# A transformer layer in split fp32: seven block products for eight also in the input projections of the two feed-forward blocks

## The chip, the cores and the metric

The kernel runs on 1 core of one Trainium2 chip. The number that counts is the device time of one execution in microseconds, the median over runs.

The layer works on 256 tokens of width 2048. Nearly all of its work is matrix products on TensorE (PE in the rows). VectorE (DVE), ScalarE (ACT), GpSimd (POOL) and SyncE (SP), which only issues DMAs here, feed it and carry its results away.

## The reference

The whole is `h + 1/2 post1(SwiGLU_1(pre1(h)))`, then a mixer with two attentions, then a second half-step feed-forward block. The change is in the first product of each SwiGLU:

```python
def swiglu_ffn(x, w_in, w_out):          # x: 256 x 2048 after RMS norm, w_in: 2048 x 11264, w_out: 5632 x 2048
    g, u = jnp.split(x @ w_in, 2, axis=-1)
    return (jax.nn.silu(g) * u) @ w_out

h = h + MACARON_W * rms_norm(swiglu_ffn(rms_norm(h, ffn1_pre_g[l]), ffn1_w_in[l], ffn1_w_out[l]), ffn1_post_g[l])
mix = hybrid_mixer(rms_norm(h, mix_pre_g[l]), w_in[l], b_gate[l], sink_a[l], rpb_b[l], w_up_a[l], w_up_b[l], w_out[l])
h = h + rms_norm(mix, mix_post_g[l])
h = h + MACARON_W * rms_norm(swiglu_ffn(rms_norm(h, ffn2_pre_g[l]), ffn2_w_in[l], ffn2_w_out[l]), ffn2_post_g[l])
```

All inputs and outputs are float32.

## The kernel before, in words

**Split products.** Each operand is split into a rounded part (fp32r, "hi") and the rest ("lo"). A product is then three matmuls: hi by hi, hi by the weights' lo, lo by the weights' hi. The weights stand as the moving operand, 512 columns wide, and 128 tokens of the activations as the stationary one. The results gather in PSUM: `acc` holds four banks of 512 columns (two column blocks, each with two token tiles), `tp` four more.

**Chunks.** A "chunk" is 128 rows of the weights by 512 columns. It costs TensorE six matmuls, three for each of the two token tiles (`half`, L1432 to L1434, called by `chunk`). A column block of the input projection takes 16 chunks. `w_in` of a feed-forward block has 22 column blocks: 11 of the gate and 11 of the up half. The kernel goes through them as 11 pairs: gate block, up block, gate block, and so on, and most pairs run inside a loop (`Fori`) on every engine.

**How a chunk gets to TensorE.** SyncE loads two chunks at a time, a "piece" of 512 KB, into one of four places of `raw`. Its wait is for VectorE to be done with the piece that lay there before. ScalarE rounds a chunk from `raw` to `WH` (`split_hi`, L650), VectorE writes `raw - WH` to `WL` (`split_lo`, L945). `WH` and `WL` have eight places each. So ScalarE can round chunk c once TensorE has finished chunk c - 8 (semaphore `chunk_done`). TensorE waits for `lo_ready` at each chunk. Every engine works its own list in order.

**Between the chunks.** ScalarE applies SiLU to the gate block (L755) and VectorE multiplies by the up block (L1099), then turns the result (L1108) into `Z`. SyncE stores `Z` to memory and fetches it back transposed as `Y`; ScalarE and VectorE split `Y` into `MH`, `ML` (L762, L1115), the operands of the output projection.

**Seven products for eight, so far.** In the output projection (`out_pair`, `superblock`) a block of 256 tokens by 256 rows by two column blocks is computed by the Strassen-Winograd scheme: seven products of a quarter block (three matmuls each, L1465 to L1467) for eight. Sums of the activations are formed by `form_sums`, sums of the weights in `T32`, and after all of them the shared products are added up on VectorE (`fold_products`, L1015, L1022).

What sets the order is written out by hand: a table for the output projection (`out_order`), plain loops for the rest.

Of the kernel before, what the change touches and what calls it, by code (L numbers as in the profile page):

```python
# [34 lines left out]
P = 128  # L35
# [72 lines left out]
C_F2OUT = C_F2IN + FFN_IN_BLOCKS * DC  # L108
# [40 lines left out]
def chunks_through(b):  # L149

    if b == B_QKV:
        return C_QKV + DC + SKEW
    if b in (B_WOUT, B_WOUT + 1):
        return C_WOUT + len(CROSSED) - 4 * (B_WOUT + 1 - b)
    for first_b, c_out in ((B_F2OUT, C_F2OUT), (B_F1OUT, C_F1OUT)):
        if first_b <= b < first_b + OUT_BLOCKS:
            return c_out + OUT_DONE[b - first_b]
    for first_b, first_c, chunks in ((B_F2IN, C_F2IN, DC), (B_WOUT, C_WOUT, DC), (B_UP, C_UP, 8),
                                     (B_QKV, C_QKV, DC), (B_F1IN, C_F1IN, DC)):
        if b >= first_b:  # L160
            return first_c + (b - first_b + 1) * chunks


def piece_of(c):

    return c // 2 if c < C_QKV else (c - EXTRA) // 2


def ops_through(piece):

    for c_out, first in ((C_F1OUT, C_F1OUT // 2), (C_F2OUT, piece_of(C_F2OUT))):
        if first <= piece < first + 2 * PAIR_PIECES:
            pair, p = divmod(piece - first, PAIR_PIECES)
            side, k, o, at = [x for x in OUT_PLACES[pair] if x[3] <= p][-1]
            return c_out + pair * PAIR_OPS + o + (4 if side == 2 else 2)
    return 2 * piece + 2 + (EXTRA if piece >= piece_of(C_QKV) else 0)


def supers_through(piece):

    count = 0
    for first in (C_F1OUT // 2, piece_of(C_F2OUT)):
        for pair in range(2):
            count += sum(side == 2 and first + pair * PAIR_PIECES + p <= piece for side, k, o, p in OUT_PLACES[pair])
    return count

# [23 lines left out]
def layer_kernel(nc, x, ffn1_pre_g, ffn1_w_in, ffn1_w_out, ffn1_post_g, mix_pre_g, w_in, b_gate,  # L210
# [4 lines left out]
    with ctx:  # L215
# [53 lines left out]
        prob = [place("prob_b", [P, TT, SEQ], F32)[0],  # L269
                place("prob_a", [P, TT, SEQ], F32, o_mask)[0]]  # L270
# [4 lines left out]
        rpad, _ = place("rpad", [B_H * RPB_USED, PADW], F32, o_yl + 8192)  # L275
# [6 lines left out]
        S32, _ = place("S32", [P, 2, 4, P], F32, o_yl + 12288)  # L282
        T32, _ = place("T32", [P, 4, NB], F32, o_xh + DC // 2 * SEQ * 4)
# [40 lines left out]

        fold = fg[:, :, :].rearrange("p t (j s) -> p (t j) s", s=NB)
# [24 lines left out]
        t_ready = sem("t_ready")  # L350

# [31 lines left out]
        def _(sp):  # L383
# [257 lines left out]
        def _(act):  # L641
# [173 lines left out]
            def ffn(c_in, c_out, b_in, b_out, z0, norm, n):  # L815
# [12 lines left out]
                else:  # L828
                    silu_gate(b_in, norm, more=SKEW)
                for c in range(DC):  # L830
                    split_hi(c_in + 2 * DC + c)
                last = DFF // NB - 1
                with act.Fori(1, last) as i:
                    for c in range(DC):
                        split_hi(c_in + DC + c, i * (2 * DC))
                        if c == 5:
                            fetched_hi(Y, z0 - 1, MH, i * 4 - 4, i)
                        if c == 8:
                            silu_gate(b_in, norm, z0, i)
# [879 lines left out]
```

## Time and profile before

| | |
|---|---|
| median of 3 runs | 2018.22 us (2017.36 to 2019.72) |
| the profiled execution | 2017.83 us, its span 2016.0 us |
| TensorE matmuls | 8866, busy 99% of the span |
| VectorE busy | 65% |
| ScalarE busy | 53% |
| mean DMA rate | 222 GB/s |
| granted TensorE clock, mean | 0.999 |

Matmuls overlap: the row of one lasts longer than the distance to the next. So TensorE's pace is read from starts, or from its weight loads (PEld) with the idle time before them, not from the busy time of the matmuls. The first feed-forward input projection runs until about 484 us.

### The profile page before, as it was taken

How to read it: one execution, taken by the hardware profiler on the slowest of the kernel's cores; microseconds unless marked ns; L12 is line 12 of the kernel's file. 1: busy time of each engine (PE TensorE's matmuls, PEld its weight loads, DVE VectorE, ACT ScalarE, POOL GpSimd, SP SyncE). 2: the span in 40 equal slices, each digit the busy share in tenths (PEclk: the TensorE clock that was granted, in tenths of full speed). 3: DMA queues.
4: the chain of work that ended last, by engine and by line, in shares of the span. 5: the costliest groups of instructions: out<-in, count | busy, mean ns of one | idle time of the engine just before them, and what ended most of it. 6: DMA issues, size and time to landing. Idle time of an engine off the chain costs nothing.

```text
span 2016.0 us, 26937 instructions
## 1 busy us (share of the span) xinstructions
PE 2005.9 (99%) x8866; PEld 1661.1 (82%) x8866; DVE 1319.4 (65%) x2059; ACT 1068.3 (53%) x1885; POOL 50.0 (2%) x86
## 2 busy tenths in 40 slices
PE   9999999999999999999999999999999999999998
PEld 7888888888888888888888888888888888888886
DVE  6655555667767776667777676765556655687685
ACT  7545555555555564445444564665555555555553
POOL 1000000000000011110000000000000000000000
PEclk9999999999999999999999999999999999999999
DMA  8787777777665678987878787586766777666564
GB/s 307 225 231 228 216 220 214 225 224 239 199 209 188 220 219 247 283 244 216 230 228 230 218 246 236 177 263 210 217 213 213 222 226 215 211 221 219 182 213 147
DMA packets 262224, 448.08 MB, mean 222 GB/s; under 512 B 17656, under 2 KB 59896, under 8 KB 261760
## 3 DMA queue, kind: packets, MB, share of 16 engines
q1 hardware_dynamic: 257520, 435.09, 70.2%
q0 software_dynamic: 4336, 11.82, 2.9%
q8 instruction: 44, 0.72, 0.1%
q14 instruction: 36, 0.29, 0.1%
q10 hardware_dynamic: 288, 0.16, 0.0%
HBM read 419.47 MB, written 27.51 MB: 222 GB/s over the span
## 4 chain that ended last, share of the span: by engine, by line
PE 98%; DMA 1%; DVE 0%; ACT 0%; SPq 0%; issue 0%; DVEq 0%; ACTq 0%
PE acc L1432 31%; PE acc L1434 31%; PE acc L1433 31%; PE tp L1466 1%; PE tp L1467 1%; PE tp L1465 1%; PE tp L1612 1%; PE tp L1625 1%; PE acc L1466 1%; PE acc L1467 1%; PE acc L1465 1%; DMA turned_blocks<-Zmix 0%; DMA raw<-in_w_out 0%; DMA raw<-in_ffn_w_in 0%; PE tp L1534 0%; DVE h L1152 0%
## 5 line engine op out<-in xcount | busy, mean ns | idle before, releaser
L945 DVE TENSOR_TENSOR WL<-raw,WH 128x512 fp32r<-128x512 f32 x1080 | 730.3, 690 | 537.5 <-ACT WH L650 536.0
L650 ACT ACTIVATE WH<-raw 128x512 fp32r<-128x512 f32 x1080 | 671.0, 630 | 691.6 <-PE acc L1434 591.0
L1432 PE MATMUL acc<-WH,XH 128*128 128x512 f32 x2030 | 794.3, 391 | 0.4 <-DVE WL L945 0.3
L1434 PE MATMUL acc<-WH,XL 128*128 128x512 f32 x2030 | 790.1, 389 | 0.0
L1433 PE MATMUL acc<-WL,XH 128*128 128x512 f32 x2030 | 790.1, 389 | 0.0
L1432 PEld LDWEIGHTS acc<-WH,XH 128*128 128x128 f32 x2030 | 381.1, 188 | 80.0 <-issue 1.1
L1434 PEld LDWEIGHTS acc<-WH,XL 128*128 128x128 f32 x2030 | 381.1, 188 | 79.3
L1433 PEld LDWEIGHTS acc<-WL,XH 128*128 128x128 f32 x2030 | 381.2, 188 | 78.7
L657 ACT ACTIVATE WH<-raw 128x512 fp32r<-128x512 f32 x312 | 188.9, 629 | 126.9 <-PE acc L1434 103.1
L952 DVE TENSOR_TENSOR WL<-raw,WH 128x512 fp32r<-128x512 f32 x280 | 183.0, 688 | 73.0 <-ACT WH L657 72.9
L1432 PE MATMUL acc<-WH,MH 128*128 128x512 f32 x560 | 217.9, 389 | 0.0
L1434 PE MATMUL acc<-WH,ML 128*128 128x512 f32 x560 | 217.9, 389 | 0.0
L1433 PE MATMUL acc<-WL,MH 128*128 128x512 f32 x560 | 217.9, 389 | 0.0
L1432 PEld LDWEIGHTS acc<-WH,MH 128*128 128x128 f32 x560 | 105.1, 188 | 22.0
L1434 PEld LDWEIGHTS acc<-WH,ML 128*128 128x128 f32 x560 | 105.1, 188 | 21.7
L1433 PEld LDWEIGHTS acc<-WL,MH 128*128 128x128 f32 x560 | 105.1, 188 | 21.8
L669 ACT ACTIVATE WH<-T 128x512 fp32r<-128x512 f32 x64 | 40.5, 632 | 61.4 <-PE acc L1434 56.4
L959 DVE TENSOR_TENSOR WL<-T,WH 128x1024 fp32r<-128x1024 f32 x32 | 39.2, 1225 | 33.7 <-ACT WH L669 33.7
L1432 PE MATMUL acc<-WH,YH 128*128 128x512 f32 x128 | 50.0, 390 | 0.0
L1433 PE MATMUL acc<-WL,YH 128*128 128x512 f32 x128 | 49.8, 389 | 0.0
L1434 PE MATMUL acc<-WH,YL 128*128 128x512 f32 x128 | 49.8, 389 | 0.0
L1108 DVE STREAM_TRANSPOSE Z<-tmp 128x512 f32<-128x512 f32 x58 | 37.9, 691 | 1.0
(158 smaller groups left out, 1072.6 us busy)
## 6 DMA issues: line engine op xcount, KB each, us to landing
raw<-in_ffn_w_in SPq DMA_DIRECT2D x350, 512.0 KB, 3.8
raw<-in_ffn_w_out SPq DMA_DIRECT2D x176, 512.0 KB, 3.9
raw<-in_w_in SPq DMA_DIRECT2D x136, 512.0 KB, 5.3
turned_blocks<-Z SPq DMA_DIRECT2D x33, 512.0 KB, 3.1
Y<-turned_blocks SPq DMA_DIRECT2D x132, 128.0 KB, 4.6
raw<-in_w_out SPq DMA_DIRECT2D x32, 512.0 KB, 4.1
raw<-in_w_up_a SPq DMA_DIRECT2D x16, 512.0 KB, 5.0
raw<-in_w_up_b SPq DMA_DIRECT2D x16, 512.0 KB, 4.6
```

Source lines behind the costliest of these rows:

```text
L650: act.activation(weight_hi(c), raw[:, piece_of(c) % RAW, c % 2, :], ACT.Copy).then_inc(hi_ready, 1)
L657: act.activation(weight_hi(op + i), raw[:, piece % RAW, i, :], ACT.Copy).then_inc(hi_ready, 1)
L669: act.activation(weight_hi(op + 4 + i), T32[:, i, :], ACT.Copy).then_inc(hi_ready, 1)
L945: dve.tensor_tensor(weight_lo(c), raw[:, piece_of(c) % RAW, c % 2, :], weight_hi(c).bitcast(F32), ALU.subtract).then_inc(lo_ready, 1)
L952: dve.tensor_tensor(weight_lo(op + i), raw[:, piece % RAW, i, :], weight_hi(op + i).bitcast(F32), ALU.subtract).then_inc(lo_ready, 1)
L959: dve.tensor_tensor(WL[:, at:at + 2, :], two, WH[:, at:at + 2, :].bitcast(F32), ALU.subtract).then_inc(lo_ready, 2)
L1432: pe.matmul(a, hi[:, tok], weight_hi(c), start=first, stop=False, skip_group_check=again)
L1433: pe.matmul(a, hi[:, tok], weight_lo(c), start=False, stop=False, skip_group_check=again)
L1434: return pe.matmul(a, lo[:, tok], weight_hi(c), start=False, stop=last, skip_group_check=again)
L1465: pe.matmul(out, hi, weight_hi(op), start=first, stop=False)
L1466: pe.matmul(out, hi, weight_lo(op), start=False, stop=False)
L1467: return pe.matmul(out, lo, weight_hi(op), start=False, stop=last)
```

## The change

The two input projections now use the seven-product scheme for 4 of the 16 chunks of each column block. A gate block and the up block of the same pair form the two column blocks, the two token tiles the rows, and chunks 0 to 3 two pairs of row chunks (`IN_S = 2`). Eight of the eleven pairs (numbers 2 to 9) are done so, in both feed-forward blocks; pairs 0, 1 and 10 stay as they were (all counted from 0).

- The products for a pair run while the up block of the pair before is computed (`mixed`, order in `MIXED`; "r" is a piece of the up block, "s" one of seven groups of two products). Then the twelve other chunks of the gate block run, then those of the up block, between which the products for the next pair stand. A round of the loop counts 40 steps of the ring of eight places (`LOOP_OPS`); the last group, T4, counts four steps for its two products.
- The shared products are chained in PSUM and not added up at the end. ScalarE copies a bank to another (`copy_bank`, five times a pair), and TensorE adds the next products onto the copy. VectorE adds once (`seed_right`) to give the up block its start.
- Weights for the products are loaded apart, four transfers of 512 KB a pair, into `SL` and `SR` (`load_sums`). VectorE forms four sums of them (`form_t`, 128x1024 each). ScalarE and VectorE split them 1024 columns at a time.
- Sums of the activations are formed once for each feed-forward block, during the gate block of pair 1.
- Two extra matmuls for each feed-forward block write the banks 1 and 2 of `tp` once.

```diff
+IN_S = 2
+LOOPS = PAIRS - 4
+B11, T2, B21, T3, B22, T1, T4 = range(7)
+MIXED = (("r", 0, 0), ("s", B11, 2), ("r", 1, 4), ("s", T2, 6), ("s", B21, 8), ("r", 2, 10), ("s", T3, 12), ("s", B22, 14),
+         ("r", 3, 16), ("s", T1, 18), ("s", T4, 20), ("r", 4, 24), ("r", 5, 26))
+GATE_OPS = 12
+MIXED_OPS = 28
+LOOP_OPS = GATE_OPS + MIXED_OPS
...
@@ sync
+            def load_sums(c, weights, block, part, di=0):
+                sp.wait_ge(lo_ready, c - 4 + LOOP_OPS * di)
+                half = part % 2 * 2
+                src = weights[bass.ds(block + part // 2 * PAIRS, 1), half:half + 2, :, :].rearrange("b c p n -> p (b c) n")
+                sp.dma_start((SL, SR)[part // 2][:, half:half + 2, :], src).then_inc(sums_landed, 16)
...
-                with sp.Fori(1, last) as i:
-                    load(c_in + DC, wi, 0, DC, i + DFF // NB, i * (2 * DC), z0, i)
-                    load(c_in + 2 * DC, wi, 0, DC, i + 1, i * (2 * DC))
+                with sp.Fori(0, LOOPS) as i:
+                    for j in range(6):
+                        load_part(piece + P_LOOP + j, wi, i + 2, 4 + 2 * j, i)
+                        if j >= 2:
+                            load_sums(c_in + O_LOOP, wi, i + 3, j - 2, i)
+                    load_mixed(piece + P_LOOP + 6, wi, i + 2 + PAIRS, z0 + 2, i)
...
@@ scalar
+            def copy_bank(done_at, out, bank, di):
+                act.wait_ge(chunk_done, done_at + LOOP_OPS * di)
+                act.activation(out, tp[:, bank, :], ACT.Copy).then_inc(copied, 1)
...
+            def mixed_hi(c, piece, d, b, norm, units, first, di=0):
+                for kind, j, o in MIXED:
+                    if o == 6:
+                        silu_gate(b, norm, units, di)
+                    if o == 10:
...
+                        copy_bank(c + 4, tp[:, 1, :], 0, di)
...
+                        copy_bank(c + 4, acc[:, left, :], 0, di)
+                    if o == 14:
+                        copy_bank(c + 8, tp[:, 2, :], 1, di)
+                    if o == 20:
+                        copy_bank(c + 14, acc[:, left + 1, :], 2, di)
+                    if o == 26:
+                        copy_bank(c + 20, TX[:, 0, :], 3, di)
...
+                        act.wait_ge(chunk_done, c + o + 2 - WS + LOOP_OPS * di)
+                        at = (c + o) % WS
+                        act.activation(WH[:, at:at + 2, :], operand(j), ACT.Copy).then_inc(hi_ready, 4 if j == T4 else 2)
...
@@ vector
+            def seed_right(c, b, d, di=0):
+                dve.wait_ge(chunk_done, c + LOOP_OPS * di)
+                dve.wait_ge(copied, 5 * (d + 1) + 5 * di)
+                dve.tensor_tensor(acc[:, 2 * (b % 2):2 * (b % 2) + 2, :], tp[:, 1:3, :],
+                                  TX[:, 0, :].unsqueeze(1).broadcast_to([P, 2, NB]), ALU.add).then_inc(seeded, 1)
...
@@ tensor
+            def products(op, group, d, b, di):
+                left = 2 * (b % 2)
+                out = {B11: tp[:, 0, :], T2: tp[:, 1, :], B21: acc[:, left, :], T3: tp[:, 2, :], B22: tp[:, 1, :], T1: tp[:, 3, :],
+                       T4: acc[:, left + 1, :]}[group]
+                if group in (T2, B21, T3, T4):
+                    pe.wait_ge(copied, 5 * d + {T2: 1, B21: 2, T3: 3, T4: 4}[group] + 5 * di)
+                if group == T1 and d:
+                    pe.wait_ge(seeded, d + di)
...
+                for bank in range(1, 3):
+                    pe.matmul(tp[:, bank, :], XH[:, 0, 0:P], weight_hi(c_in + O_MIXED1 - 4), start=True, stop=True)
...
+                with pe.Fori(0, LOOPS) as i:
+                    for j in range(6):
+                        piece(c_in + O_LOOP + 2 * j, b_in + 4, 4 + 2 * j, False, j == 5, i, True)
+                    mixed(c_in + O_LOOP + GATE_OPS, b_in + 5, first + 1, True, i)
```

On TensorE, at the border from the gate block to the up block of a loop round, first before, then of the change a little further on: the group B11 after the first piece of the up block, and the group T2. `tp<-WH,XH` is a product's matmul, `copied` the semaphore of ScalarE's bank copies.

```order
L1525 ISA
L1438 REGISTER_ALU [waits acc_freed0]
L1432 MATMUL acc<-WH,XH 128x512 [waits lo_ready]
L1433 MATMUL acc<-WL,XH 128x512
L1434 MATMUL acc<-WH,XL 128x512
L1432 MATMUL acc<-WH,XH 128x512
L1433 MATMUL acc<-WL,XH 128x512
```
```order
L1662 REGISTER_ALU
L1663 MATMUL tp<-WH,XH 128x512 [waits lo_ready]
L1664 MATMUL tp<-WL,XH 128x512
L1665 MATMUL tp<-WH,XL 128x512
L1662 REGISTER_ALU
L1663 MATMUL tp<-WH,XH 128x512 [waits lo_ready]
L1664 MATMUL tp<-WL,XH 128x512
L1665 MATMUL tp<-WH,XL 128x512
L1673 ISA
L1662 REGISTER_ALU [waits copied]
L1663 MATMUL tp<-WH,MH 128x512 [waits lo_ready]
L1664 MATMUL tp<-WL,MH 128x512
```

Before, a chunk's six matmuls follow each other and the only other wait is for a free bank. Now there are products with three matmuls and a wait of their own, and T2 also waits for ScalarE.

On ScalarE, in the loop around SiLU, first before, then of the change from T2's weights to T3's. `WH<-TX` and `WH<-SL` are the rounding of two chunks of weights at once, `tp<-tp` and `acc<-tp` the bank copies.

```order
L650 ACTIVATE WH<-raw 128x512 [waits chunk_done]
L753 REGISTER_ALU [waits rstd_ready,chunk_done]
L755 ACTIVATE tmp<-acc,rstd 128x512 [waits blocks_turned]
L755 ACTIVATE tmp<-acc,rstd 128x512
L649 REGISTER_ALU
L650 ACTIVATE WH<-raw 128x512 [waits chunk_done]
L649 REGISTER_ALU [waits raw_landed1]
```
```order
L802 ACTIVATE WH<-TX 128x1024 [waits chunk_done,x_ready]
L800 REGISTER_ALU
L802 ACTIVATE WH<-SL 128x1024 [waits chunk_done]
L783 REGISTER_ALU
L772 REGISTER_ALU [waits seeded]
L773 ACTIVATE tp<-tp 128x512 [waits chunk_done]
L785 REGISTER_ALU
L773 ACTIVATE acc<-tp 128x512 [waits chunk_done,acc_freed0]
L753 REGISTER_ALU
L755 REGISTER_ALU [waits raw_landed0]
L756 ACTIVATE WH<-raw 128x512 [waits chunk_done] x2
```

Before, SiLU stands between single chunks. Now each copy stands in ScalarE's list ahead of the rounding of later weights, and waits for TensorE's products.

On VectorE, in the loop around the gate product, first before, then of the change. `TX<-SR,SL` is `form_t` of T1, `acc<-tp,TX` is `seed_right`.

```order
L945 TENSOR_TENSOR WL<-raw,WH 128x512 [waits hi_ready]
L1096 REGISTER_ALU [waits chunk_done]
L1099 SCALAR_TENSOR_TENSOR tmp<-acc,rstd,tmp 128x512 [waits rstd_ready,acc_freed0]
L1099 SCALAR_TENSOR_TENSOR tmp<-acc,rstd,tmp 128x512
L1108 STREAM_TRANSPOSE Z<-tmp 128x4x4x32 [waits acc_freed1]
L1108 STREAM_TRANSPOSE Z<-tmp 128x4x4x32
L944 REGISTER_ALU
L945 TENSOR_TENSOR WL<-raw,WH 128x512 [waits hi_ready]
```
```order
L1272 SCALAR_TENSOR_TENSOR tmp<-acc,rstd,tmp 128x512 [waits rstd_ready,acc_freed0]
L1272 SCALAR_TENSOR_TENSOR tmp<-acc,rstd,tmp 128x512
L1281 STREAM_TRANSPOSE Z<-tmp 128x4x4x32 [waits acc_freed1]
L1281 STREAM_TRANSPOSE Z<-tmp 128x4x4x32
L1119 ISA [waits chunk_done]
L1120 TENSOR_TENSOR acc<-tp,TX 128x1024 [waits copied]
L1095 TENSOR_TENSOR WL<-raw,WH 128x512 [waits hi_ready]
L1095 TENSOR_TENSOR WL<-raw,WH 128x512 [waits hi_ready]
L1107 ISA
L1109 REGISTER_ALU [waits sums_landed]
L1114 TENSOR_TENSOR TX<-SR,SL 128x1024 [waits seeded]
L1114 TENSOR_TENSOR TX<-SR,TX 128x1024 [waits x_ready]
```

The gate product, which stood in the middle of a gate block, now stands after its eighth chunk, followed by the addition into the up block's banks and by the two sums, of which the first waits for the four transfers (`sums_landed`).

## Rows read from the trace of the kernel before

**Rows 1.** The page, part 1: busy us, share of the span, instructions.
```profile
PE 2005.9 (99%) x8866; PEld 1661.1 (82%) x8866; DVE 1319.4 (65%) x2059; ACT 1068.3 (53%) x1885; POOL 50.0 (2%) x86
```

**Rows 2.** Waits of TensorE, whole span: total us, times, longest us.
```profile
PE tp L1635 <- POOL ident L566: 1.5, 1, 1.5
PE acc L1543 <- ACT WH L650: 0.8, 1, 0.8
PE acc L1432 <- DVE WL L945: 0.3, 1, 0.3
```

**Rows 3.** The page, part 4: the chain that ended last, by engine.
```profile
PE 98%; DMA 1%; DVE 0%; ACT 0%; SPq 0%; issue 0%; DVEq 0%; ACTq 0%
```

**Rows 4.** Groups by form, weight loads: busy us, mean ns, idle before them.
```profile
L1433 PEld LDWEIGHTS acc<-WL,XH 128*128 128x128 f32 x2030 | 381.2, 188 | 78.7
L1432 PEld LDWEIGHTS acc<-WH,XH 128*128 128x128 f32 x2030 | 381.1, 188 | 80.0 <-issue 1.1 <-DVE WL L945 0.7
...
L1465 PEld LDWEIGHTS tp<-WH,XH 128*128 128x128 f32 x48 | 9.0, 188 | 1.9
```

**Rows 5.** Timeline of TensorE where superblocks begin: start us, us, what.
```profile
507.05 0.39 PE L1465 MATMUL tp<-WH,MH 128*128 128x512 f32 x1
...
507.73 0.39 PE L1465 MATMUL acc<-WH,MH 128*128 128x512 f32 x1
```

**Rows 6.** Window 484 to 560 us: busy us and counts, clock, DMA share, GB/s.
```profile
484.00:560.00 76.00, 76.00 (x337) 62.98 (x336) 58.73 (x80) 43.82 (x72) 0.58 (x1) 1.00 0.67 217
```

**Rows 7.** Timeline of VectorE in the first loop: start us, us, what [idle before].
```profile
186.15 1.85 DVE L945 TENSOR_TENSOR WL<-raw,WH 128x512 fp32r<-128x512 f32 x3
...
195.12 0.69 DVE L945 TENSOR_TENSOR WL<-raw,WH 128x512 fp32r<-128x512 f32 x1 [0.67 <-ACT WH L650]
196.48 0.69 DVE L945 TENSOR_TENSOR WL<-raw,WH 128x512 fp32r<-128x512 f32 x1 [0.67 <-ACT WH L650]
```

**Rows 8.** Timeline of ScalarE in the first loop.
```profile
204.51 1.25 ACT L755 ACTIVATE tmp<-acc,rstd 128x512 f32<-128x512 f32 x2
```

**Rows 9.** Groups by form, VectorE and ScalarE.
```profile
L945 DVE TENSOR_TENSOR WL<-raw,WH 128x512 fp32r<-128x512 f32 x1080 | 730.3, 690 | 537.5 <-ACT WH L650 536.0
L650 ACT ACTIVATE WH<-raw 128x512 fp32r<-128x512 f32 x1080 | 671.0, 630 | 691.6 <-PE acc L1434 591.0 <-DMA raw<-in_w_in 49.7 <-DMA raw<-in_ffn_w_in 31.3
...
L1108 DVE STREAM_TRANSPOSE Z<-tmp 128x512 f32<-128x512 f32 x58 | 37.9, 691 | 1.0
L1099 DVE SCALAR_TENSOR_TENSOR tmp<-acc,rstd,tmp 128x512 f32<-128x512 f32 x44 | 30.9, 744 | 0.0
...
L967 DVE TENSOR_TENSOR T<-raw 128x1024 f32<-128x1024 f32 x16 | 19.6, 1223 | 16.8 <-DMA raw<-in_ffn_w_out 16.8
...
L1015 DVE TENSOR_TENSOR acc<-acc,fg 128x1024 f32<-128x1024 f32 x4 | 4.9, 1226 | 0.0
...
L868 ACT ACTIVATE YH<-tp 128x256 fp32r<-128x256 f32 x16 | 5.2, 365 | 0.7 <-PE tp L1625 0.7
...
L674 ACT ACTIVATE XH<-S 128x1024 fp32r<-128x1024 f32 x4 | 4.2, 1046 | 0.0
...
L680 ACT ACTIVATE fg<-tp 128x512 f32<-128x512 f32 x4 | 2.3, 581 | 0.0
```

**Rows 10.** Waits of ScalarE over the whole span.
```profile
ACT WH L650 <- DMA raw<-in_ffn_w_in: 31.3, 23, 3.7
```

**Rows 11.** Waits of SyncE's DMA queue over the whole span.
```profile
SPq L387 <- DVE Z L1108: 99.6, 29, 7.0
```

**Rows 12.** Windows, as rows 6: the start, the first loop, ten busy microseconds.
```profile
14.00:30.00 16.00, 16.00 (x72) 13.24 (x72) 10.93 (x20) 12.51 (x30) 0.00 (x0) 1.00 1.06 388
43.60:479.00 435.40, 435.40 (x1923) 360.68 (x1922) 259.28 (x388) 221.51 (x362) 6.98 (x9) 1.00 0.76 221
190.00:200.00 10.00, 10.00 (x46) 8.29 (x45) 5.22 (x8) 4.53 (x8) 0.79 (x1) 1.00 1.03 287
```

**Rows 13.** The page, part 6: DMA issues, KB each, median us to landing.
```profile
raw<-in_ffn_w_in SPq DMA_DIRECT2D x350, 512.0 KB, 3.8
```

More of the change, by code:

```diff
@@ L185, in supers_through, with j_step @@
     return count
+def j_step(group):
+    return {T1: 1, T2: 2, T3: 3, T4: 4}[group]
 def in_second_ring(c):
@@ L1215, in ffn @@
                     if c == 8:
[L1216 to L1226 removed]
+                        gate_times_up(b_out - 3, norm)
@@ new lines, in products @@
+            def products(op, group, d, b, di):
+                left = 2 * (b % 2)
+                out = {B11: tp[:, 0, :], T2: tp[:, 1, :], B21: acc[:, left, :], T3: tp[:, 2, :], B22: tp[:, 1, :], T1: tp[:, 3, :],
[4 more added lines that the diff above has]
+                    pe.wait_ge(seeded, d + di)
+                fresh = group in (B11, T1)
+                for q in range(IN_S):
+                    first, second = XH[:, 2 * q, :], XH[:, 2 * q + 1, :]
+                    first_lo, second_lo = XL[:, 2 * q, :], XL[:, 2 * q + 1, :]
+                    sh, sl = in_sum(MH, q), in_sum(ML, q)
+                    hi, lo = {B11: (first[:, 0:P], first_lo[:, 0:P]), T2: (sh[:, 1, :], sl[:, 1, :]),
+                              B21: (second[:, 0:P], second_lo[:, 0:P]), T3: (sh[:, 2, :], sl[:, 2, :]),
+                              B22: (sh[:, 3, :], sl[:, 3, :]), T1: (sh[:, 0, :], sl[:, 0, :]),
+                              T4: (second[:, P:2 * P], second_lo[:, P:2 * P])}[group]
+                    last = q == IN_S - 1
+                    product(out, op + q, hi, lo, fresh and q == 0, last, di, not fresh).then_inc(
+                        chunk_done, 3 if group == T4 and last else 1)
@@ new lines, in piece, with mixed @@
+            def piece(c, b, k, first, last, di=0, again=False):
+                for i in range(2):
+                    chunk(c + i, b, XH[:, k + i, :], XL[:, k + i, :], first and i == 0, last and i == 1, LOOP_OPS * di, again)
+            def mixed(c, b, d, again, di=0):
+                for kind, j, o in MIXED:
+                    if kind == "s":
+                        products(c + o, j, d, b - 1, di)
+                    else:
+                        if j == 0 and again:
+                            pe.wait_ge(seeded, d + di)
+                        piece(c + o, b, 4 + 2 * j, False, j == 5, di, again)
@@ new lines, in ffn @@
+                for j in range(12):
+                    if j == 6:
+                        pe.wait_ge(seeded, first + LOOPS + 1)
+                    piece(c_in + O_PAIR9 + 2 * j, b_in + j // 6, 4 + 2 * (j % 6), False, j % 6 == 5, 0, True)
+                for side in range(2):
+                    acc_free(b_out - 2 + side)
+                    for c in range(DC):
+                        chunk(c_in + O_PAIR10 + side * DC + c, b_out - 2 + side, XH[:, c, :], XL[:, c, :], c == 0, c == DC - 1)
```

322 lines of the change are left out of this document (221 added, 101 removed).

## The prediction

> **What bounds the kernel now.** I read the page's totals first: TensorE is busy 99% of the span with 8866 matmuls, VectorE 65%, ScalarE 53% [rows 1]. Busy time of matmuls overlaps, so I looked next at what TensorE waited for: 2.6 us in all, in three waits, all near the start [rows 2]. The chain that ended last is 98% TensorE [rows 3]. So the kernel is one unbroken stream of matmuls, and what counts is their number times their distance. The distance comes from the weight loads: (381.2 + 78.7) us over 2030 loads, 0.2266 us each [rows 4]. VectorE's timeline agrees: it follows TensorE chunk by chunk, and two chunks lie 1.36 us apart, six matmuls of 0.2267 us [rows 7]. The reader is to see that VectorE and ScalarE are idle only because they are ahead: both wait for each other or for TensorE (537.5 and 691.6 us of idle time at the splitting of chunks) [rows 9].
>
> **The change, its saving.** A pair of column blocks cost 32 chunks of 6 matmuls, 192. Now it costs 24 chunks of 6 and 14 products of 3, that is 144 + 42 = 186. Six fewer in 8 pairs of 2 feed-forward blocks are 96; two extra in each block give 4 back. Net 92, which is also the difference of the matmuls in the two programs when loop bodies are counted with their rounds: 8866 against 8774. The saving is 96 x 0.2267 = 21.76 us, less 4 x 0.2267 = 0.91 us: 20.85 us. All of it lies on the path that sets the end, provided that TensorE never has to wait for the new steps.
>
> **Does a product keep the distance of 0.2267 us?** It has a wait, and in the loop a register step, for every three matmuls instead of six. Superblocks in the output projection have the same shape: two products start 0.68 us apart, three times 0.227 [rows 5], and their loads give (9.0 + 1.9) / 48 = 0.227 us [rows 4]. The register step is not in those. Chunks in the loop have one in front of the load at L1432, and these loads idled 80.0 us against 78.7 for L1433 [rows 4]. That is 1.3 us over some 1015 waits, 1.3 ns each. 224 new products at that price are 0.3 us; I take 0 and keep 0.3 as the upper end.
>
> The Trainium skill (TensorE: Matmul & The Clock Gate, "The cost: per-tile semaphore tail") says that semaphore increments by matmuls serialize at about 26 ns each. By that rule the six more increments of a pair would cost, as an estimate, 16 x 6 x 0.026 = 2.5 us. The rows of the superblocks show no such lengthening, though each product there increments once, so the sum goes by the rows.
>
> **Do the new steps stay hidden?** I walk one round of the loop. M 0 is the start of the up block on TensorE, where the products for the next pair are mixed in. TensorE's starts follow from 2.72 us for a piece of two chunks and 1.36 us for a group of two products: B11 at 2.72, T2 at 6.80, B21 at 8.16, T3 at 12.24, B22 at 13.60, T1 at 17.68, T4 at 19.04, the last two pieces at 20.40 and 23.12, the next gate block at 25.84, its end at 42.16. A matmul ends 0.16 us after its slot (row of 0.39 us, distance 0.23 [rows 5]); I take 0.2 us until another engine moves.
>
> ScalarE's steps: a chunk 0.63 us (about 0.57 in a row), SiLU 1.25 us for two tiles [rows 8], two chunks of weights at once 1.05 us, a copy out of PSUM 0.58 us [rows 9]. Its list: SiLU until 1.5, T2's weights until 2.5, B21's until 4.0 (it waits for the ring), then B11 is done at 4.3 and the two copies run until 5.4. T2 needs the first at 6.80: hidden. T3's weights until 8.1, third copy (T2 done at 8.4) until 8.9, needed at 12.24. T1's weights until 13.5, fourth copy until 14.4, needed at 19.04; T4's weights until 15.5. Chunks of piece 4: 16.5 to 17.2 and 17.9 to 18.5. Fifth copy (T1 done at 19.2) until 19.8, then the chunks of the last piece at 20.4 and 21.0.
>
> VectorE's steps: 1.22 us for 1024 columns, 0.69 for 512, 0.58 in a row ((1.85 - 0.69) / 2 [rows 7, 9]). The weights' lo are ready: T2 at 3.7, B21 5.2, T3 9.1, B22 11.0, T1 14.8, T4 16.8, piece 4 at 17.9 and piece 5 at 21.2. TensorE wants them at 6.80, 8.16, 12.24, 13.60, 17.68, 19.04, 20.40 and 23.12. The least lead is 1.9 us, at piece 5, because T4 takes four of the eight places of the ring for two products and the fifth copy waits in front of piece 5.
>
> In the gate block (G 0 = M 25.84) VectorE is done with the eighth chunk at G 1.6, then gate product and turning (2 x 0.744 + 2 x 0.691 less overlap, 2.7 us), `seed_right` 1.23 us (as L1015 [rows 9]), two chunks, T1 at G 6.8 to 8.0, two chunks until 9.3, T2's sum until 10.5. TensorE wants the ninth chunk at G 10.9 and the eleventh at 13.6. So what is added on VectorE, about 33 us busy in a round of 42.2, is covered by the ring's lead of eight chunks, 10.9 us.
>
> A copy from PSUM to PSUM by ScalarE is in no row. Bounds: 0.37 us (256 columns from PSUM) and 1.23 us (VectorE, 1024 columns into PSUM) [rows 9]; I take 0.58, the copy of 512 columns to SBUF. At 1.23 the least lead falls to 1.3 us, still no wait. A gain is excluded, since no step of the kernel before goes away with it. In the gate block of pair 1 VectorE also forms the sums of activations (1.22 + 4 x 0.43 us and waits, about 3.2, then 1.22 for their lo). With the rest that is 19.4 of 21.8 us, with the lead of the ring before it: hidden, and in the worst case 1 or 2 us once for each feed-forward block.
>
> **DMAs.** The bytes are the same. But the four transfers of weights for the products are bunched: SyncE's waits free pieces 2 to 5 of the gate block and the four parts between M 19.5 and 25.2. A transfer of 512 KB takes 1.35 us at the 388 GB/s that the start reached; landing takes 3.8 us from issue [rows 12, 13], so 2.45 us lie around it. Eight in a row from 19.6: two until 22.3, six more until 30.4, landed at 32.9, which is G 7.1. T1's sum wants them at 6.8 and can be late until 11.7 before TensorE waits for the eleventh chunk. In the stretch with the relative-position transfers the rate was 287 GB/s [rows 12]: 1.83 us each, landed at G 10.9, still in time. ScalarE did wait for pieces before, up to 3.7 us [rows 10], and TensorE never noticed. The queue's waits for `Z` (99.6 us in 29 [rows 11]) stay, and now stand where pieces are 10 us ahead.
>
> **The sum.** 2017.83 (the profiled execution, span 2016.0) - 21.76 + 0.91 = 1996.98 us. The median of the runs shown is 0.39 us above the profiled one, so 1997.4 us.
>
> **Rivals.**
> - *Small waits in the rounds.* The leads of 1.9 to 2.9 us are eaten here and there, by 0.5 to 1 us in each of 14 loop rounds: +7 to +14 us, 2004 to 2011 us. For it: the walk has three engines and a queue in step, and five copies that wait for products. Against it: every lead is over 1.2 us at the upper bounds. 9 in 100.
> - *The bunched transfers decide, slower than before.* Place: T1's sum on VectorE. At the loop's mean of 221 GB/s [rows 12] each transfer takes 2.37 us, the last lands at G 15.1, and the eleventh chunk is 3.4 us late: 14 x 3.4 = 48 us, about 2045 us. It turns the gain into a loss from 1.49 us a round (20.85 / 14), when a transfer takes 2.12 us, 247 GB/s. Against it: 221 GB/s was the demand, at 0.76 of the engines' time, and not the limit. 5 in 100.
> - *Products run at a longer distance.* With the register step and wait not hidden, 224 products at 10 to 30 ns: +2 to +7 us, 2000 to 2004 us. Against it: rows 4 and 5. 3 in 100.
> - *The clock falls.* Between groups in changing banks TensorE would pause, and the granted clock drop to 1.2 GHz. If the 114 matmuls of each mixed stretch ran so, 16 x 114 x 0.2267 = 413 us more, 2411 us. Against it: in the stretch with superblocks, which go through seven banks, the clock was 1.00 and TensorE had no gap [rows 6]. 1 in 100. The Trainium skill (TensorE: Matmul & The Clock Gate, "A second HAM failure mode: psum-queue depth-cycling") describes this for a kernel that cycles through banks; by that rule the trace disagrees for this kernel.
> - That fewer matmuls go than stated is excluded by the count.
>
> **How the numbers follow.** The forecast has 82 in 100: 1997.4 us, with 1995.5 to 1999.5 from the spread of runs (2017.36 to 2019.72) and the 0.3 us of register steps. To hold 8 in 10 with the parts of the first and third rival that lie near, I let the range reach to 2005. A change under 0.2%, 4 us, can't be told from none here. Faster: 82, 3 and nearly all of 9, and a little less for what I don't see, 0.93; within 0.2%: 0.02; slower: the second and the fourth, 0.05.
>
> **What would show it.** Right: 8774 matmuls; no wait of TensorE on `copied`, `seeded` or `lo_ready` in the loops beyond a few tenths; rounds of 42.2 us, which VectorE's timeline shows between two gate products; ScalarE's copies near 0.58 us; VectorE busy about 33 us of a round. Wrong: idle time before product matmuls on TensorE released by ScalarE (the copies) or VectorE (T1, T4, piece 5); VectorE idle before T1's sum on a DMA for more than 5 us; a granted clock under 1.00; rounds of 43.5 us or more.

## The result and the profile after

The changed kernel takes 1996.88 us (median of 4 runs, 1996.7 to 1999.51) against 2018.22 us before (4 runs, 2017.36 to 2019.72). The ratio is 0.9897, its 95% interval 0.9879 to 0.9914. Forecast were 1997.4 us and a gain of 20.85 us; the medians differ by 21.3 us, the spans of the profiled executions by 21.1 us (2016.0 to 1994.9).

The totals of the profile after, against [rows 1]:

```profile
PE 1985.8 (100%) x8774; PEld 1645.1 (82%) x8774; DVE 1441.5 (72%) x2135; ACT 1127.6 (57%) x1951; POOL 50.1 (3%) x86
```

There are 92 matmuls fewer (8866 to 8774), as counted ahead. VectorE is 122 us busier and ScalarE 59 us, and neither shows in the time. What TensorE waited for, all of it, against [rows 2]:

```profile
PE tp L1878 <- POOL ident L665: 1.5, 1, 1.5
```

One wait is left, at the very start. The two short ones beside it in [rows 2], 1.1 us together, are not there in this execution; they are too small to explain anything: the gain by spans is only 0.25 us above the forecast one, and two executions differ by more (a second profile of the same kernel has a span of 1995.3 us).

The weight loads, from which the pace is read, against [rows 4]; L1630 and L1631 are the plain chunks, L1663 the products, with busy us, mean ns and idle time before them:

```profile
L1631 PEld LDWEIGHTS acc<-WL,XH 128*128 128x128 f32 x1774 | 333.1, 188 | 68.5
L1630 PEld LDWEIGHTS acc<-WH,XH 128*128 128x128 f32 x1774 | 333.1, 188 | 69.1 <-issue 0.5
...
L1663 PEld LDWEIGHTS tp<-WH,MH 128*128 128x128 f32 x144 | 27.0, 188 | 5.6
```

The chunks: (333.1 + 68.5) / 1774 = 0.2264 us, as before. The products: (27.0 + 5.6) / 144 = 0.226 us. So a product with a wait and a register step for every three matmuls keeps the pace.

The new steps, groups by form of the same profile, against [rows 9]:

```profile
L802 ACT ACTIVATE WH<-SL 128x1024 fp32r<-128x1024 f32 x48 | 50.8, 1059 | 25.5 <-PE acc L1632 25.5
...
L1120 DVE TENSOR_TENSOR acc<-tp,TX 128x1024 f32<-128x1024 f32 x16 | 19.2, 1201 | 0.0
...
L773 ACT ACTIVATE tp<-tp 128x512 f32<-128x512 f32 x32 | 18.6, 582 | 7.6 <-PE tp L1665 7.6
L773 ACT ACTIVATE acc<-tp 128x512 f32<-128x512 f32 x32 | 18.5, 580 | 3.8 <-PE tp L1665 3.8
...
L773 ACT ACTIVATE TX<-tp 128x512 f32<-128x512 f32 x16 | 9.6, 598 | 11.6 <-PE tp L1665 11.6
```

ScalarE's copy from PSUM to PSUM took 0.58 us, the value taken from the copy to SBUF; `seed_right` took 1.20 us for 1.23.

One round of the loop on ScalarE, from its timeline: SiLU of one round, the fifth copy, the chunks of piece 5 and of the next gate block, SiLU of the next round.

```profile
204.56 1.27 ACT L890 ACTIVATE tmp<-acc,rstd 128x512 f32<-128x512 f32 x2 [2.17 <-PE acc L1632]
...
223.52 0.60 ACT L773 ACTIVATE TX<-tp 128x512 f32<-128x512 f32 x1 [0.73 <-PE tp L1665]
224.01 3.22 ACT L756 ACTIVATE WH<-raw 128x512 fp32r<-128x512 f32 x6
...
246.72 1.27 ACT L890 ACTIVATE tmp<-acc,rstd 128x512 f32<-128x512 f32 x2 [2.17 <-PE acc L1632]
```

Two SiLUs lie 246.72 - 204.56 = 42.16 us apart, which is 186 x 0.2267. With SiLU taken as 0.2 us behind the start of the up block, M 0 of the prediction is 204.36 (the block's first matmul stands at 204.28, so places read in this way are good to 0.1 us), and the fifth copy starts at M 19.2, as walked. VectorE in the same round:

```profile
224.67 4.91 DVE L1095 TENSOR_TENSOR WL<-raw,WH 128x512 fp32r<-128x512 f32 x8 [1.15 <-ACT WH L756]
...
232.14 1.40 DVE L1272 SCALAR_TENSOR_TENSOR tmp<-acc,rstd,tmp 128x512 f32<-128x512 f32 x2
...
234.81 1.20 DVE L1120 TENSOR_TENSOR acc<-tp,TX 128x1024 f32<-128x1024 f32 x1
...
237.68 1.22 DVE L1114 TENSOR_TENSOR TX<-SR,SL 128x1024 f32<-128x1024 f32 x1 [0.49 <-DMA SR<-in_ffn_w_in]
238.82 1.29 DVE L1095 TENSOR_TENSOR WL<-raw,WH 128x512 fp32r<-128x512 f32 x2
```

The first of the eight chunks at 224.67 is that of piece 5. Its lo is ready at 225.36, M 21.0; TensorE wants it at M 23.12. The lead is 2.1 us, forecast 1.9. The gate block starts at 204.36 + 25.84 = 230.20, so the gate product stands at G 1.9, T1's sum at G 7.5 after 0.49 us of waiting for the last of the four transfers (forecast: landed at G 7.1), and the eleventh chunk is ready at 239.5, G 9.3, 4.3 us ahead of G 13.6. The burst of transfers is plain in two windows of the same stretch, the DMA share and GB/s last, against [rows 12]:

```profile
208.00:226.00 18.00, 18.00 (x81) 14.93 (x80) 13.70 (x18) 13.49 (x22) 0.79 (x1) 1.00 0.37 80
226.00:242.00 16.00, 16.00 (x72) 13.24 (x72) 14.12 (x21) 7.75 (x14) 0.00 (x0) 1.00 1.03 383
```

### The profile page after: what moved, and what is told of

Same layout as the page of the kernel before. It is cut to its first block, busy times and chain, and to the rows that moved or that the text cites. A ratio compares the mean times of both kernels' runs of the same rounds, so it can differ in the third digit from the quotient of the medians.

```text
span 1994.9 us, 26750 instructions
## 1 busy us (share of the span) xinstructions
PE 1985.8 (100%) x8774; PEld 1645.1 (82%) x8774; DVE 1441.5 (72%) x2135; ACT 1127.6 (57%) x1951; POOL 50.1 (3%) x86
## 4 chain that ended last, share of the span: by engine, by line
PE 100%; DVE 0%; DVEq 0%; ACT 0%; issue 0%; POOL 0%; ACTq 0%; POOLq 0%
PE acc L1630 29%; PE acc L1632 29%; PE acc L1631 29%; PE tp L1665 3%; PE tp L1663 3%; PE tp L1664 3%; PE acc L1665 1%; PE acc L1663 1%; PE acc L1664 1%; PE tp L1868 1%; PE tp L1855 1%; PE tp L1878 0%; PE tp L1769 0%; DVE h L1325 0%; PE acc L1778 0%; PE tp L1828 0%
## 5 line engine op out<-in xcount | busy, mean ns | idle before, releaser
L1630 PE MATMUL acc<-WH,XH 128*128 128x512 f32 x1774 | 694.3, 391 | 0.0
L1632 PE MATMUL acc<-WH,XL 128*128 128x512 f32 x1774 | 690.4, 389 | 0.0
L1631 PE MATMUL acc<-WL,XH 128*128 128x512 f32 x1774 | 690.3, 389 | 0.0
L756 ACT ACTIVATE WH<-raw 128x512 fp32r<-128x512 f32 x760 | 448.7, 627 | 322.1 <-PE acc L1632 184.7
L1095 DVE TENSOR_TENSOR WL<-raw,WH 128x512 fp32r<-128x512 f32 x728 | 469.3, 687 | 158.8 <-ACT WH L756 158.4
L1088 DVE TENSOR_TENSOR WL<-raw,WH 128x512 fp32r<-128x512 f32 x504 | 336.9, 688 | 219.5 <-ACT WH L749 218.2
L749 ACT ACTIVATE WH<-raw 128x512 fp32r<-128x512 f32 x504 | 309.3, 628 | 312.2 <-PE acc L1632 228.8
L1632 PEld LDWEIGHTS acc<-WH,XL 128*128 128x128 f32 x1774 | 333.0, 188 | 69.2
L1630 PEld LDWEIGHTS acc<-WH,XH 128*128 128x128 f32 x1774 | 333.1, 188 | 69.1 <-issue 0.5
L1631 PEld LDWEIGHTS acc<-WL,XH 128*128 128x128 f32 x1774 | 333.1, 188 | 68.5
L1630 PE MATMUL acc<-WH,MH 128*128 128x512 f32 x560 | 217.8, 389 | 0.0
L1631 PE MATMUL acc<-WL,MH 128*128 128x512 f32 x560 | 217.8, 389 | 0.0
L1630 PEld LDWEIGHTS acc<-WH,MH 128*128 128x128 f32 x560 | 105.1, 188 | 21.8
L1631 PEld LDWEIGHTS acc<-WL,MH 128*128 128x128 f32 x560 | 105.1, 188 | 21.7
L1102 DVE TENSOR_TENSOR WL<-SL,WH 128x1024 fp32r<-128x1024 f32 x48 | 58.7, 1224 | 21.4 <-ACT WH L802 21.4
L802 ACT ACTIVATE WH<-SL 128x1024 fp32r<-128x1024 f32 x48 | 50.8, 1059 | 25.5 <-PE acc L1632 25.5
L1663 PE MATMUL tp<-WH,MH 128*128 128x512 f32 x144 | 56.0, 389 | 0.0
```

What stands on the lines that cost most here:

```text
L749: act.activation(weight_hi(c), raw[:, piece_of(c) % RAW, c % 2, :], ACT.Copy).then_inc(hi_ready, 1)
L756: act.activation(weight_hi(op + i), raw[:, piece % RAW, i, :], ACT.Copy).then_inc(hi_ready, 1)
L802: act.activation(WH[:, at:at + 2, :], operand(j), ACT.Copy).then_inc(hi_ready, 4 if j == T4 else 2)
L1088: dve.tensor_tensor(weight_lo(c), raw[:, piece_of(c) % RAW, c % 2, :], weight_hi(c).bitcast(F32), ALU.subtract).then_inc(lo_ready, 1)
L1095: dve.tensor_tensor(weight_lo(op + i), raw[:, piece % RAW, i, :], weight_hi(op + i).bitcast(F32), ALU.subtract).then_inc(lo_ready, 1)
L1630: pe.matmul(a, hi[:, tok], weight_hi(c), start=first, stop=False, skip_group_check=again)
```

## The experiments

Every experiment computes the whole layer.

**Six matmuls put back (fill_six).** The first B11 product and the first T1 product of each pair are issued twice; the first time is overwritten by the second.

```diff
                     last = q == IN_S - 1
+                    if fresh and q == 0:
+                        product(out, op + q, hi, lo, True, True, di, False)
                     product(out, op + q, hi, lo, fresh and q == 0, last, di, not fresh).then_inc(
```

Expected: 

> The changed kernel with its first B11 product and its first T1 product of each pair issued twice: 6 matmuls more a pair, 96 in all, nothing else new. The theory (the gain is the number of matmuls times 0.2267 us): 1996.9 + 96 x 0.2267 = 2018.7 us, the time of before and the two extra matmuls a block. Rival (part of the gain came from waits that went or from slack that TensorE would fill): less than half of that, under 2008 us.

```profile
PE 2006.7 (100%) x8870; PEld 1661.9 (82%) x8870; DVE 1443.6 (72%) x2135; ACT 1127.2 (56%) x1951; POOL 50.1 (2%) x86
```

Measured: 2018.4 us (10 runs), ratio to the kernel before 1.0007 (0.9997 to 1.0016); 8870 matmuls, span 2016.6 us. 96 matmuls cost 21.7 us of span, 0.226 us each, and the whole gain is gone although every other part of the change is in place. So the gain is the count; nothing else in the change has a share in it that these runs could show.

**A wait and an increment for each half chunk (before_halves).** The kernel before, with the shape of the products' synchronization in its plain chunks (1079 of them by the calls of `chunk`; the expectation said some 900).

```diff
-                pe.wait_ge(lo_ready, c + 1 + more)
                 for t in range(TT):
+                    pe.wait_ge(lo_ready, c + 1 + more)
                     mm = half(c, b, t, hi, lo, first, last)
+                    if t == 0:
+                        mm.then_inc(halves, 1)
                 mm.then_inc(chunk_done, 1)
```

Expected: 

> The kernel before, with each plain chunk's wait repeated ahead of its second token tile and a semaphore incremented by the last matmul of the first tile, as products have them: a wait every three matmuls instead of six in some 900 chunks. The theory (a wait and an increment for three matmuls cost nothing): 2018.2 us, within 1 us. Rival (the increment lengthens the stream by 26 ns, the Trainium skill, TensorE: Matmul & The Clock Gate, the cost: per-tile semaphore tail): as an estimate some 900 x 0.026 = 23 us, 2041 us. Rival of 10 ns: 2027 us.

The diff adds no register step, so this run tests the wait and the increment alone. The weight loads of its chunks, groups by form:

```profile
L1434 PEld LDWEIGHTS acc<-WL,XH 128*128 128x128 f32 x2030 | 381.2, 188 | 78.4
L1433 PEld LDWEIGHTS acc<-WH,XH 128*128 128x128 f32 x2030 | 381.1, 188 | 80.2 <-issue 1.5
```

Measured: 2017.41 us, ratio 0.9999 (0.9989 to 1.0008). The idle time before the loads stayed at 78.4 and 80.2 us, against 78.7 and 80.0 in [rows 4]. A wait and a semaphore increment for every three matmuls cost nothing measurable in this stream; the register step of a product is covered by the products' own loads above. By the rule of the Trainium skill (TensorE: Matmul & The Clock Gate, "The cost: per-tile semaphore tail") 1079 increments would have cost an estimated 28 us; the page fits that figure to the tail behind a group of tiles, and this run shows that it can't be carried into this unbroken stream.

**The fifth copy repeated, two and five times (copy_plus2, copy_plus5).** This eats the least lead of the walk, at piece 5. The diff is that of five; for two, both fives are twos.

```diff
+                        act.wait_ge(chunk_done, c + 20 + LOOP_OPS * di)
+                        for k in range(5):
+                            act.activation(TX[:, 0, :], tp[:, 3, :], ACT.Copy).then_inc(repeated, 1)
+                            act.wait_ge(repeated, 5 * d + k + 1 + 5 * di)
                         copy_bank(c + 20, TX[:, 0, :], 3, di)
```

Expected of two: 

> The fifth bank copy of ScalarE (into TX) preceded by two more of the same in every pair: about 1.3 us more on ScalarE in front of piece 5, whose least lead was worked out at 1.9 us. The theory (leads as walked): hidden, 1996.9 us, no wait of TensorE. Rival (leads are eaten by things that the walk leaves out): TensorE waits some tenths in each of 16 stretches, 2000 to 2010 us.

Measured: 1997.29 us, ratio 0.9901 (0.9885 to 0.9918), span 1994.9 us, exactly that of the changed kernel. Hidden, but for one wait of 0.2 us.

Expected of five: 

> Five more of these copies, about 3.2 us on ScalarE in front of piece 5. The theory: more than the lead of 1.9 to 2.1 us, so TensorE waits 1.1 to 1.3 us at the first chunk of piece 5 in each of 16 stretches: +18 to +21 us, 2015 to 2018 us, all the waiting at that place. Rival (the ring's lead is larger than walked, since other steps absorb it): under 2003 us.

ScalarE's timeline in one round, and TensorE's waits in the whole span (total us, times, longest):

```profile
228.03 3.13 ACT L795 ACTIVATE TX<-tp 128x512 f32<-128x512 f32 x5 [0.73 <-PE tp L1670]
231.18 0.60 ACT L774 ACTIVATE TX<-tp 128x512 f32<-128x512 f32 x1
```

```profile
PE acc L1635 <- DVE WL L1100: 16.2, 16, 1.0
```

The matmuls on both sides of one of these waits:

```profile
231.68 0.39 PE L1637 MATMUL acc<-WH,XL 128*128 128x512 f32 x1
233.08 0.50 PE L1635 MATMUL acc<-WH,XH 128*128 128x512 f32 x1 [1.01 <-DVE WL L1100]
233.41 0.39 PE L1636 MATMUL acc<-WL,XH 128*128 128x512 f32 x1
```

Measured: 2019.18 us (10 runs), ratio 1.0006 (0.9997 to 1.0016). Five copies took 3.13 us, 1.0 more than the lead of 2.1, and TensorE waited at the predicted place, 16 times, one for each pair, at most 1.0 us by its matmuls and 1.4 us by its weight loads. The kernel lost 22.3 us, 1.4 us a pair. That is more than the 18 to 21 us expected: the expectation took the loss of a pair as the copies less the lead. The starts show 1.40 us where 0.23 is usual, and 0.33 us behind the first matmul after the wait, 1.3 us lost in these two distances. The lead is real, and it is short: 3.1 us of ScalarE a pair at this one place in the order cost as much as the whole change gives.

**The four transfers behind SyncE's wait for Z (sums_late).** They are issued in `load_mixed`, after its second piece.

```diff
                     for j in range(6):
                         load_part(piece + P_LOOP + j, wi, i + 2, 4 + 2 * j, i)
-                        if j >= 2:
-                            load_sums(c_in + O_LOOP, wi, i + 3, j - 2, i)
...
-                    load_mixed(piece + P_LOOP + 6, wi, i + 2 + PAIRS, z0 + 2, i)
+                    load_mixed(piece + P_LOOP + 6, wi, i + 2 + PAIRS, z0 + 2, i, c_in + O_LOOP, i + 3)
...
+                    if j == 1 and sums is not None:
+                        for part in range(4):
+                            load_sums(sums, weights, sums_block, part, di)
```

Expected: 

> In the 14 loop rounds the four transfers of weights for the products are issued behind the second piece of the up block, and so behind SyncE's wait for Z, and no longer between pieces 2 to 5 of the gate block. The bytes stay. The theory (T1's sum on VectorE must start by G 11.7, counted from the start of the gate block, before TensorE waits for the eleventh chunk): issued from G 5.4 on, the last part lands at about 5.9 + 4 x 1.35 + 2.45 = G 13.8, TensorE waits some 2.1 us before the eleventh chunk in 14 rounds, +29 us, 2024 to 2028 us, VectorE idle before T1's sum on the DMA. Rival (transfers are hidden in any case, as ScalarE's waits for pieces are): under 2000 us.

SyncE's queue and VectorE in one round, from the timelines, and the waits of TensorE's loads:

```profile
205.34 0.37 SPq L452 DMA_DIRECT2D turned_blocks<-Z  x1
205.97 0.37 SPq L544 DMA_DIRECT2D raw<-in_ffn_w_in  x1
206.61 1.10 SPq L551 DMA_DIRECT2D SL<-in_ffn_w_in  x2
207.92 0.93 SPq L551 DMA_DIRECT2D SR<-in_ffn_w_in  x2
```

```profile
202.57 1.40 DVE L1273 SCALAR_TENSOR_TENSOR tmp<-acc,rstd,tmp 128x512 f32<-128x512 f32 x2
...
216.26 1.23 DVE L1115 TENSOR_TENSOR TX<-SR,SL 128x1024 f32<-128x1024 f32 x1 [8.64 <-DMA SR<-in_ffn_w_in]
217.40 1.28 DVE L1096 TENSOR_TENSOR WL<-raw,WH 128x512 fp32r<-128x512 f32 x2
```

```profile
PEld acc L1631 <- DVE WL L1096: 60.6, 14, 7.5
```

Measured: 2077.55 us, ratio 1.0295 (1.0277 to 1.0313), far more than expected. The place was right: 14 waits, one for each round, released by VectorE's splitting as expected; in the round shown the wait stands before the eleventh chunk. The size was not, for two reasons. First, the store of `Z` and a piece go into the queue just ahead of the four parts (205.34 and 205.97). By the prediction's arithmetic six transfers of 1.35 us from 205.4 end at 213.5, and 2.45 us later it is 216.0. T1's sum starts at 216.26, G 15.4 (the gate block's first matmul is at 200.82), and the eleventh chunk starts at 218.14, 3.7 us behind its place at 214.42. The expectation had counted four transfers. Two of the waits are longer, 5.7 us in the first round and 7.0 us in the sixth; why was not looked into. Second, the clock fell behind the wait:

```profile
214.19 0.39 PE L1633 MATMUL acc<-WH,XL 128*128 128x512 f32 x1
218.14 0.54 PE L1631 MATMUL acc<-WH,XH 128*128 128x512 f32 x1 [3.56 <-DVE WL L1096]
218.48 0.63 PE L1632 MATMUL acc<-WL,XH 128*128 128x512 f32 x1
218.91 0.63 PE L1633 MATMUL acc<-WH,XL 128*128 128x512 f32 x1
```

```profile
212.00:220.00 8.00, 4.44 (x17) 3.33 (x16) 3.74 (x5) 2.10 (x3) 0.00 (x0) 0.90 0.94 295
220.00:224.00 4.00, 4.00 (x15) 3.15 (x15) 4.00 (x6) 1.13 (x2) 0.00 (x0) 0.77 0.77 226
224.00:232.00 8.00, 8.00 (x37) 6.64 (x36) 6.48 (x7) 6.38 (x10) 0.79 (x1) 1.00 0.55 108
```

After 3.56 us without a matmul the next ones start 0.43 us apart and not 0.227, for some 3.4 us: the granted clock is 0.90 and 0.77 in these windows, and 1.00 after. This is TensorE's lower level, 1.2 GHz of 2.4. The span grew by 80.3 us, of which 60.6 us are waits. Windows around the 14 waits show a clock under 1.00 in 13 of them; 3.4 us at half pace lose 1.7 us, so 13 such stretches are about 22 us, near the 19.7 us that are left (the mean granted clock of the run is 0.987).

One wait of the same run, in the second feed-forward block, is nearly as long and nothing slows behind it:

```profile
1537.49 0.50 PE L1631 MATMUL acc<-WH,XH 128*128 128x512 f32 x1 [3.24 <-DVE WL L1096]
1537.83 0.40 PE L1632 MATMUL acc<-WL,XH 128*128 128x512 f32 x1
```

```profile
1536.00:1544.00 8.00, 6.51 (x29) 5.40 (x30) 8.00 (x11) 4.64 (x7) 0.00 (x0) 1.00 0.87 196
```

Two waits as short in the first block (3.2 and 3.1 us, windows 262 to 270 and 308 to 318 us) have clocks of 0.79 and 0.83. So a wait of this length can bring the lower clock, and need not. What decides is not shown.

**Three reductions more on VectorE before T1's sum (form_plus).**

```diff
+                if group == T1:
+                    for k in range(3):
+                        dve.reduce_max(extra[:, k:k + 1], SR[:, 2 * (k % 2):2 * (k % 2) + 2, :].rearrange("p a b -> p (a b)"), AX.X)
                 dve.tensor_tensor(operand(group), x, y, ALU.subtract).then_inc(x_ready, 1)
```

Expected: 

> Three reductions over 1024 columns of SR on VectorE ahead of T1's sum in each of 16 pairs, some 3.3 us more of VectorE's time in a gate block. The theory (the lead at the eleventh chunk is 4.3 us): hidden, 1996.9 us, VectorE some 53 us busier in all. Rival (VectorE, busy 33 of 42.2 us in a round, is near to being the bound): 16 waits of 0.5 us or more, over 2005 us.

TensorE's waits, its matmuls behind the longest, and VectorE in the first round of the first loop:

```profile
PE acc L1634 <- DVE WL L1096: 3.9, 3, 3.3
```

```profile
121.08 0.50 PE L1634 MATMUL acc<-WH,XH 128*128 128x512 f32 x1 [3.27 <-DVE WL L1096]
121.42 0.39 PE L1635 MATMUL acc<-WL,XH 128*128 128x512 f32 x1
```

```profile
109.52 1.40 DVE L1276 SCALAR_TENSOR_TENSOR tmp<-acc,rstd,tmp 128x512 f32<-128x512 f32 x2
...
115.82 3.47 DVE L1117 TENSOR_REDUCE extra<-SR 128x1 f32<-128x1024 f32 x3 [1.26 <-DMA SR<-in_ffn_w_in]
119.21 1.22 DVE L1118 TENSOR_TENSOR TX<-SR,SL 128x1024 f32<-128x1024 f32 x1
120.34 1.29 DVE L1096 TENSOR_TENSOR WL<-raw,WH 128x512 fp32r<-128x512 f32 x2
```

Measured: 2002.07 us (4 runs, three within 0.6 us and one at 2007.02), ratio 0.9931 (0.9913 to 0.9948), 4.9 us slower than the changed kernel on the same chip (1997.15 us, below). Neither theory had it. In the rounds of the steady loop 3.4 us were hidden, as expected of the lead of 4.3 us, but for waits of a few tenths. But one wait of 3.3 us (3.7 us by the loads) stands in the first round, and one of 0.4 us (0.9) in the gate block of pair 1: 4.6 us by the loads, about the whole loss. Behind the wait of 3.3 us the matmuls went on 0.23 us apart, at a clock of 1.00. The first round of the changed kernel itself, on VectorE, shows why:

```profile
108.67 1.41 DVE L1272 SCALAR_TENSOR_TENSOR tmp<-acc,rstd,tmp 128x512 f32<-128x512 f32 x2
...
114.76 1.23 DVE L1114 TENSOR_TENSOR TX<-SR,SL 128x1024 f32<-128x1024 f32 x1 [1.04 <-DMA SR<-in_ffn_w_in]
115.90 1.29 DVE L1095 TENSOR_TENSOR WL<-raw,WH 128x512 fp32r<-128x512 f32 x2
```

SiLU of this round stands at 120.24, so its gate block starts at 103.72, and the gate product that is at G 1.9 in the steady round is at G 5.0 here. T1's sum starts at G 11.0 and the eleventh chunk is ready at 116.6, G 12.9, where TensorE wants it at 13.6. The lead is 0.7 us, not 4.3. The pieces with chunks 5 to 8 of the gate block came late: ScalarE rounds them at 103.70 and 106.79, G 0.0 and 3.1, and in the steady round at 227.56 and 230.26, G -2.6 and 0.1. The transfers of the relative positions (issued at 93.2 us) and one long issue on SyncE's queue (2.75 us at 97.87) stand before it. Which of the two made the pieces late was not tried. The first round of the second feed-forward block, where no such transfers or long issue stand, is late too, but less: its gate product is at G 3.6 (1385.63), its eleventh chunk ready at G 10.7, so the lead there is 2.9 us.

**Pair 10 too (nine_pairs), beside the changed kernel once more (after_again).** A ninth round of mixed products stands behind the loop, and pair 10 has 12 chunks a block. The fetched block of pair 8 lies where `SL` and `SR` are, so it is split only in pair 10.

```diff
-O_PAIR10 = O_PAIR9 + 2 * GATE_OPS
-IN_OPS = O_PAIR10 + 2 * DC
+O_PAIR10 = O_PAIR9 + LOOP_OPS
+IN_OPS = O_PAIR10 + 2 * GATE_OPS
...
+                mixed(c_in + O_PAIR9 + GATE_OPS, b_in + 1, first + 1 + LOOPS, True)
+                for j in range(12):
+                    if j == 6:
+                        pe.wait_ge(seeded, first + LOOPS + 2)
+                    piece(c_in + O_PAIR10 + 2 * j, b_in + j // 6, 4 + 2 * (j % 6), False, j % 6 == 5, 0, True)
```

Expected: 

> Pair 10 is done by the seven products too: nine pairs of eleven. A ninth round of mixed products stands behind the loop; the fetched block of pair 8 is split only after it, since its place is SL's and SR's. 6 matmuls fewer a feed-forward block, 12 in all: 8762. The theory (each matmul is worth 0.2267 us and the leads hold): 2.7 us less than the changed kernel, 1994.2 us. Rival (the new round waits once for a late split or for the fetched block, some 3 us a block): no better than the changed kernel, 1996.9 us or more.

Expected of the changed kernel: 

> The changed kernel unchanged, beside nine_pairs on the same chip: 1996.9 us, and its ratio to the kernel before again 0.990. If the theory and the rival of nine_pairs lie 2.7 us apart, its spread of some 0.3 us over the fast runs must be small enough to tell them apart.

```profile
PE 1983.3 (100%) x8762; PEld 1642.3 (82%) x8762; DVE 1455.6 (73%) x2143; ACT 1135.1 (57%) x1959; POOL 50.0 (3%) x86
```

```profile
PE tp L1883 <- POOL ident L670: 1.5, 1, 1.5
```

Measured on the same chip: 1994.77 us (1993.85 to 1995.89, 4 runs) against 1997.15 us (1997.04 to 1997.69, 4 runs). The ratios to the kernel before are 0.9888 (0.9871 to 0.9906) and 0.990 (0.9882 to 0.9917). The intervals overlap, the runs do not; the medians differ by 2.4 us and the spans by 2.8 us (1992.5 and 1995.3), for the 2.7 us that 12 matmuls are worth. No wait by the matmuls is new (the loads show two of 0.3 and 0.4 us). This is the fastest version of the study.

## Why the prediction was right

- **What bounds the kernel.** One stream of matmuls at 0.2267 us, their number times this distance: right, and shown from both sides, by `fill_six` (96 more, +21.7 us) and `nine_pairs` (12 fewer, -2.8 us by the spans, -2.4 by the medians).
- **The pace of products.** Taken as unchanged; measured 0.226 us. The rival of 10 to 30 ns a product fell with the loads of the profile after, and for the wait and the increment with `before_halves` too.
- **The walk through a round.** Period 42.16 us as worked out, fifth copy at M 19.2, lead at piece 5 2.1 us (forecast 1.9), T1's sum at G 7.5 (forecast 7.1), lead at the eleventh chunk 4.3 us. `copy_plus2` and `copy_plus5` showed the first lead from both sides. VectorE's time in a round was put at 33 us; in the round from 204.36 to 246.52 it was busy 32.9 us.
- **The copy from PSUM to PSUM,** bounded by 0.37 and 1.23 us and taken as 0.58 us: 0.58 us.
- **The bunched transfers.** That late transfers hold up T1's sum, and with it TensorE, is real and dear, as `sums_late` shows. But the rival's condition, a lower rate, was not met: in the burst (226 to 242 us above) the DMA engines moved 383 GB/s, and 388 was taken.
- **The first rival, small waits in the rounds,** did not come. The first round is the exception that the prediction missed. It took the leads of the steady loop for all rounds, and granted only that 1 or 2 us might be lost in the gate block of pair 1, and that in the stretch with the relative-position transfers the last part would land at G 10.9; in the first round T1's sum did start at G 11.0. In the first round the lead was 0.7 us, found only when `form_plus` overdrew it. The forecast held there by 0.7 us, with some luck.
- **The clock** stayed at 1.00 through the change of banks, so the rival fell. In the experiments the clock went down behind 13 of the 14 waits of `sums_late`, and not behind one of 3.2 us there nor behind that of 3.3 us in `form_plus`. The prediction's price for late transfers (48 us) left the clock out, and the expectation for `sums_late` with it.
- **Two readings that were off, with nothing resting on them.** Of the three waits in [rows 2] the one of 0.3 us does not stand near the start but between 1000 and 1320 us. And of the 691.6 us that ScalarE was idle ahead of its splitting [rows 9], 81 us were waits for DMAs, not for VectorE or TensorE.

## What to carry to other kernels

When the profile shows an engine without a gap, count its instructions before and after and take the difference times their distance; then walk one round of the other engines against the times at which that engine wants its operands, and write down the least lead with its place. Walk the first round too, with the transfers of the start in it, since the leads there can be a fraction of those in the steady loop. When a transfer is moved behind a wait, count everything that enters the queue with it.

## What the runs showed of the hardware

- A semaphore wait and an increment for every three matmuls of 512 columns cost nothing measurable: 1079 more of each, 2017.41 against 2017.59 us (medians of 10 and 25 runs).
- ScalarE copied 512 columns of fp32 from PSUM to PSUM in 580 to 582 ns and to SBUF in 581 ns (`fg`, [rows 9]) and 598 ns (`TX`), so the target made no clear difference. TensorE accumulated onto the copied banks at its full pace (0.226 us a matmul).
- A pause of TensorE of 3.56 us was followed by matmuls 0.43 us apart for some 3.4 us before the distance of 0.227 us came back; pauses of 3.24 us (`sums_late`) and 3.27 us (`form_plus`) were not.
- Queued transfers of 512 KB ran at 383 GB/s from 226 to 242 us, 1.37 us each (524,288 B / 383 GB/s); in the 18 us before, when little was issued, the same engines moved 80 GB/s.
